# First norm's operands at the head of the weight queue, one branch around the overflow passes, and a two-pass last norm, in a four-layer fp32 network on one core

## The reference, cut to what matters

```python
# block 1, layer 0 begins with
h = x * rsqrt(mean(x * x) + 1e-6) * pre_mix_norm[0]     # first norm, 256 x 1024
proj = h @ w_in[0]                                       # 2464 columns
...
# block 2, layer 1 ends with (ALPHA = 4 ** 0.25)
top_val, top_idx = top_k(h @ router, 2)                  # 8 experts, 2 per token
gate = one_hot(top_idx) weighted by softmax(top_val)
y = 0
for e in range(8):
    y += gate[:, e] * ((silu(h @ w_gate[e]) * (h @ w_up[e])) @ w_down[e])   # 1024 -> 3584 -> 1024
z = ALPHA * h + y
out = (z - mean(z)) * rsqrt(var(z) + 1e-5) * ln_g + ln_b
```

## Time and profile before

| | |
|---|---|
| three executions, median | 2643.1 us (2642.37, 2643.1, 2655.18) |
| profiled execution | 2652.31 us, its span 2650.5 us |
| mean granted TensorE clock | 0.958 |
| PE, PEld, DVE, ACT, POOL busy | 93%, 51%, 18%, 15%, 4% |
| moved by DMA | 568 MB, mean 214 GB/s |
| the expert layer in the span | 1640 to 2618 us |

### The profile page before, as it was taken

The page is one execution under the profiler, slowest core; times in us unless marked ns, Lnnn a source line. Parts: engine busy times, 40 slices in busy tenths (PEclk is TensorE's granted clock), DMA queues, the critical chain, the costliest instruction groups (busy, mean ns, idle before and its releaser), DMA issues. The chain is left out here.

```text
span 2650.5 us, 34369 instructions
## 1 busy us (share of the span) xinstructions
PE 2475.4 (93%) x14986; PEld 1340.9 (51%) x14987; DVE 488.7 (18%) x1219; ACT 398.8 (15%) x967; POOL 110.3 (4%) x189
## 2 busy tenths in 40 slices
PE   6899999999999599999977997999999999999994
PEld 3577774678774264867546744333333333333331
DVE  2340004240001441200102513111111110101112
ACT  0420001330000142100011521111111111011110
POOL 3110000000000020000000100000000000000000
PEclk9999999799999789999975998999999999999997
DMA  8558543433343244243433233999999999999991
GB/s 268 196 65 213 199 143 118 178 105 137 133 145 113 68 136 174 104 161 109 130 103 123 70 136 130 357 384 355 350 354 391 334 358 367 359 368 357 367 361 54
DMA packets 247242, 568.11 MB, mean 214 GB/s; under 512 B 10224, under 2 KB 25776, under 8 KB 247088
## 3 DMA queue, kind: packets, MB, share of 16 engines
q1 hardware_dynamic: 234992, 531.71, 55.0%
q0 software_dynamic: 12096, 34.12, 5.8%
HBM read 556.62 MB, written 9.18 MB: 213 GB/s over the span
## 5 line engine op out<-in xcount | busy, mean ns | idle before, releaser
L1241 PE MATMUL ps_d<-slots,hT 128*32 128x512 f32 x3584 | 391.8, 593 | 0.1
L867 PE MATMUL ps_a<-slots,hT 128*128 128x512 f32 (+4 forms) x672 | 276.4, 569 | 17.6 <-ACT hT L1477 9.9
L1241 PEld LDWEIGHTS ps_d<-slots,hT 128*32 128x32 f32 x3584 | 112.7, 110 | 257.5 <-issue 257.1
L1268 PE MATMUL ps_x<-slots,PT 128*32 128x512 f32 x1792 | 213.0, 593 | 0.8 <-ACT PT L1633 0.8
L867 PEld LDWEIGHTS ps_a<-slots,hT 128*128 128x128 f32 x672 | 127.1, 196 | 160.1 <-issue 145.0
L1241 PE MATMUL ps_s<-slots,hT 128*32 128x512 f32 x1792 | 197.4, 592 | 0.0
L1054 PE MATMUL ps_a<-hT,slots 128*128 128x256 f32 x864 | 191.0, 379 | 1.9 <-issue 1.9
L1054 PE MATMUL ps_d<-hT,slots 128*128 128x256 f32 x864 | 190.9, 379 | 0.0
L1054 PEld LDWEIGHTS ps_a<-hT,slots 128*128 128x128 f32 x864 | 163.8, 190 | 29.5 <-issue 8.0
L1054 PEld LDWEIGHTS ps_d<-hT,slots 128*128 128x128 f32 x864 | 164.2, 190 | 22.3
L2278 DVE TENSOR_TENSOR proj<-proj,ps_d 128x512 f32<-128x512 f32 x33 | 22.7, 687 | 595.4 <-PE ps_d L1054 521.4
(11 more groups left out here) (350 smaller groups left out, 2263.8 us busy)
## 6 DMA issues: line engine op xcount, KB each, us to landing
slots<-in_moe_w_gate SPq DMA_DIRECT2D x56, 2048.0 KB, 9.6
slots<-in_moe_w_up SPq DMA_DIRECT2D x56, 2048.0 KB, 10.6
slots<-in_moe_w_down SPq DMA_DIRECT2D x56, 2048.0 KB, 11.2
slots<-in_ffn_w_gate_up SPq DMA_DIRECT2D x20, 2048.0 KB, 9.7
slots<-in_ffn_w_down SPq DMA_DIRECT2D x10, 2048.0 KB, 8.4
slots<-in_w_in SPq DMA_DIRECT2D x8, 2048.0 KB, 9.7
slots<-in_ff_w_gate SPq DMA_DIRECT2D x5, 2048.0 KB, 7.9
slots<-in_ff_w_up SPq DMA_DIRECT2D x5, 2048.0 KB, 7.8
```

Source lines behind the costliest of these rows:

```text
L867: last = pe.matmul(b[:, 0:c], lhs[:, k, t * P:(t + 1) * P], v[:, k, :], start=(k == 0), stop=(k == s["k"] - 1))
L1241: last = pe.matmul(b[TILE * j:TILE * j + TILE, :], x_of[i][:, k, TILE * c:TILE * c + TILE], views[w][:, k, :], start=(k == 0), stop=(k == ...
L1268: last = pe.matmul(b0[TILE * j:TILE * j + TILE, :], mine(f + o, c), v[:, f + o, 512 * half:512 * half + 512], start=(first and o == 0), st ...
```

## The change

Four edits. (1) SP issues the first norm's gain between the two tiles of x, with a semaphore of its own; GpSimd keeps only the identity ahead of a wait for weight block 0, and issues all its tables behind that wait. (2) BODY becomes 1; the count read is the maximum over the eight experts, and one branch stands around a loop of eight turns, so that either all experts run both overflow passes or none does. (3) O begins as ALPHA X instead of zero; this is written behind the counts instead of ahead of them. (4) `last_norm` takes its statistics straight from O, of both tiles before the first normalising pass, and does the rest in two passes of 512-column halves, (O - mean) * gain and then * inverse root + shift; SP stores each half when it is done.

```diff
-BODY = 2
+BODY = 1
...
+        most = loads[0:1, EXPERTS:EXPERTS + 1]          # loads is one column wider
...
             for t in range(T):                            # SP
                 sp.dma_start(X[:, t, :], a["x"][0, t * P:(t + 1) * P, :])...
+                if t == 0:
+                    sp.dma_start(vec[:, 0, :], vectors[0].unsqueeze(0).broadcast_to([P, D])).then_inc(
+                        *lane.tick(first_vec_landed, ("vec", 0), by=16))
...
-                with lane.loop(sp, 2) as turn:
-                    for u in range(BODY):
-                        ...
-                        n = sp.value_load(loads[0:1, bass.ds(e, 1)], min_val=0, max_val=S)
-                        with sp.If(n > FIRST):
-                            for groups in passes:
-                                expert(e, groups)
-                        with sp.Else():
-                            ...
+                start = dict(lane.count)
+                n = sp.value_load(most, min_val=0, max_val=S)
+                with sp.If(n > FIRST):
+                    with lane.loop(sp, 2) as e:
+                        for groups in s["groups"]:
+                            expert(e, groups)
+                with sp.Else():
+                    added = {sem.name: count for sem, count in lane.since(start)}
+                    for n in range(s["first"] - SLOTS, s["first"]):
+                        landed = slot_landed[n % SLOTS]
+                        sp.wait_ge(*lane.of(("weights", n)))
+                        sp.sem_inc(landed, added[landed.name])
             for t in range(T):
-                sp.wait_ge(*lane.of(("last", t)))
-                sp.dma_start(out[0, t * P:(t + 1) * P, :], X[:, t, :])...
+                for c in (0, 512):
+                    sp.wait_ge(*lane.of(("last", t, c)))
+                    sp.dma_start(out[0, t * P:(t + 1) * P, c:c + 512], X[:, t, c:c + 512])...
...
                 pool.dma_start(ident[:, :], a["c_ident"])...
-                pool.dma_start(vec[:, 0, :], vectors[0].unsqueeze(0).broadcast_to([P, D]))...
+                pool.wait_ge(*lane.of(("weights", 0)))
                 for dst, src in ((onehot, a["c_bucket"]), ...
...
             def last_norm(s):
-                g, b = use_vec(s["gain"]), use_vec(s["shift"])
+                g, shift = use_vec(s["gain"]), use_vec(s["shift"])
                 dve.wait_ge(*lane.own())
-                for t in range(T):
-                    do(dve.scalar_tensor_tensor(X[:, t, :], X[:, t, :], ALPHA, O[:, t, :], ALU.mult, ALU.add))
+
+                def moments(t):
                     for c in range(2):
-                        do(dve.bn_stats(stat[:, 36 + 6 * c:42 + 6 * c], X[:, t, 512 * c:512 * c + 512]))
+                        do(dve.bn_stats(stat[:, 36 + 6 * c:42 + 6 * c], O[:, t, 512 * c:512 * c + 512]))
                     do(dve.bn_aggr(stat[:, 32 + 2 * t:34 + 2 * t], stat[:, 36:48]))
-                    inv_root(1, stat[:, 33 + 2 * t:34 + 2 * t], 1.0, LN_EPS)
-                    do(dve.tensor_scalar(X[:, t, :], X[:, t, :], stat[:, 32 + 2 * t:33 + 2 * t], stat[:, 0:1],
-                                         ALU.subtract, ALU.mult))
-                    do(dve.tensor_tensor(X[:, t, :], X[:, t, :], g, ALU.mult), ("vec_used", s["gain"]))
-                    do(dve.tensor_tensor(X[:, t, :], X[:, t, :], b, ALU.add), ("vec_used", s["shift"]), ("last", t))
+
+                moments(0)
+                r = start_root(1, stat[:, 33:34], 1.0, LN_EPS)
+                moments(1)
+                for t in range(T):
+                    for c in (0, 512):
+                        o, x = O[:, t, c:c + 512], X[:, t, c:c + 512]
+                        post(dve.scalar_tensor_tensor(x, o, stat[:, 32 + 2 * t:33 + 2 * t], g[:, c:c + 512],
+                                                      ALU.subtract, ALU.mult), ("vec_used", s["gain"]))
+                    end_root(1, r)
+                    for c in (0, 512):
+                        x = X[:, t, c:c + 512]
+                        post(dve.scalar_tensor_tensor(x, x, stat[:, 0:1], shift[:, c:c + 512], ALU.mult, ALU.add),
+                             ("vec_used", s["shift"]), ("last", t, c))
+                    if t == 0:
+                        dve.wait_ge(*lane.own())
+                        r = start_root(1, stat[:, 35:36], 1.0, LN_EPS)
...
-                do(dve.memset(O[:, :, :], 0.0))
                 b, n = bank(lane, "d")                     # route_tokens
                 dve.wait_ge(*lane.of(("full", "d", n)))
...
-                do(dve.tensor_copy(loads[:, :], b[:, 16:24]), ("free", "d", n), ("loads", 0), sem=d_free)
+                do(dve.tensor_copy(loads[:, 0:EXPERTS], b[:, 16:24]))
+                do(dve.tensor_reduce(loads[:, EXPERTS:EXPERTS + 1], b[:, 16:24], AX, ALU.max), ("free", "d", n),
+                   ("loads", 0), sem=d_free)
+                for t in range(T):
+                    post(dve.tensor_scalar(O[:, t, :], X[:, t, :], ALPHA, None, ALU.mult))
...
                 elif kind == "experts":                    # VectorE; TensorE and ScalarE likewise
-                    with lane.loop(dve, 2) as turn:
-                        for u in range(BODY):
-                            start, before = dict(lane.count), lane.own()
-                            tokens = dve.value_load(loads[0:1, bass.ds(turn * BODY + u, 1)], min_val=0, max_val=S)
-                            with dve.If(tokens > FIRST):
-                                for first, groups in zip(s["starts"], s["groups"][2 * u:2 * u + 2]):
-                                    expert(groups, first, turn * BODY + u)
-                            with dve.Else():
-                                dve.wait_ge(*before)
-                                for sem, count in lane.since(start):
-                                    dve.sem_inc(sem, count)
+                    start, before = dict(lane.count), lane.own()
+                    tokens = dve.value_load(most, min_val=0, max_val=S)
+                    with dve.If(tokens > FIRST):
+                        with lane.loop(dve, 2) as e:
+                            for first, groups in zip(s["starts"], s["groups"]):
+                                expert(groups, first, e)
+                    with dve.Else():
+                        dve.wait_ge(*before)
+                        for sem, count in lane.since(start):
+                            dve.sem_inc(sem, count)
```

More of the change, by code:

```diff
@@ L1429, in _ @@
                 elif kind == "experts":
-                    with lane.loop(pe, 2) as turn:
-                        for u in range(BODY):
-                            start, before = dict(lane.count), lane.own()
[L1433 to L1438, removed]
-                                for sem, count in lane.since(start):
-                                    pe.sem_inc(sem, count)
+                    start, before = dict(lane.count), lane.own()
+                    tokens = pe.value_load(most, min_val=0, max_val=S)
+                    with pe.If(tokens > FIRST):
+                        with lane.loop(pe, 2) as e:
+                            for groups in s["groups"]:
+                                expert(groups)
+                    with pe.Else():
+                        pe.wait_ge(*before)
+                        for sem, count in lane.since(start):
+                            pe.sem_inc(sem, count)
                 elif kind == "route":
@@ L1739, in _ @@
                 elif kind == "experts":
-                    with lane.loop(act, 2) as turn:
-                        for u in range(BODY):
-                            start, before = dict(lane.count), lane.own()
-                            tokens = act.value_load(loads[0:1, bass.ds(turn * BODY + u, 1)], min_val=0, max_val=S)
-                            with act.If(tokens > FIRST):
-                                for groups in s["groups"][2 * u:2 * u + 2]:
-                                    expert(groups)
-                            with act.Else():
-                                act.wait_ge(*before)
-                                for sem, count in lane.since(start):
-                                    act.sem_inc(sem, count)
+                    start, before = dict(lane.count), lane.own()
+                    tokens = act.value_load(most, min_val=0, max_val=S)
+                    with act.If(tokens > FIRST):
+                        with lane.loop(act, 2) as e:
+                            for groups in s["groups"]:
+                                expert(groups)
+                    with act.Else():
+                        act.wait_ge(*before)
+                        for sem, count in lane.since(start):
+                            act.sem_inc(sem, count)
                 leave(lane, n)
```

26 lines of the change are left out of this document (7 added, 19 removed).

## The result

The changed kernel takes **2630.8 us** in the median of 13 executions (2618.2 to 2645.2), the kernel before 2643.1 in 13 (2640.8 to 2660.3). The measured ratio is 0.9924 with a 95% interval of 0.9904 to 0.9944, so it is faster, by 0.76% in this measure. This ratio, like those of the experiments, is not the quotient of the two medians, which is 0.9953 here. The forecast was 2619.7, with a range of 2612 to 2632. The profiled execution takes 2631.24, its span is 2629.4; before they were 2652.31 and 2650.5. Span against span that is -21.1 us, median against median -12.3. The difference between these two is the main thing to explain.

The account below looks back on a forecast made before the run. TensorE was taken to bound the expert layer, so only start, routing and end could change: -8.0 + 1.8 - 12.0 - 4.6 - 0.6 = -23.4 us off the median of 2643.1, giving 2619.7 us, range 2612 to 2632.

Parts of the forecast that it names:

- Rival (b): Whole kernel: the changed median falls with the highest executions, 2631.8 us, not told from no change; chance 0.10.
- Start: Kernel start: with the tables behind weight block 0, that block lands at 13.0 us and TensorE starts earlier, -8.0 us.
- The cover for GpSimd: After the start: GpSimd's tables and biases shift by 10.5 us, and a further delay below 14 us costs nothing.
- rival (d): Start: the tables slow weight block 1, TensorE stands again after the first product, 4 us, 2623.7 us; chance 0.05.
- Routing: Ahead of the experts' gather: a reduction and two scalings added behind the counts, +1.8 us.
- 1 more: Routing: 1 us more if half of TensorE's longer standing cost again as slow matmuls.
- rival (c): Routing into expert layer: TensorE's clock stays low longer, for 60 us giving 2649.7 us, so slower; chance 0.03.
- Branches: End, VectorE's loop of empty experts: one turn left instead of eight, the norm starts earlier, -12.0 us.
- norm: Last norm: statistics of both tiles, then eight passes over 512 columns, 9.4 us instead of 14.01, -4.6 us.
- tail: After the last norm, final store: the last piece is 256 KB instead of 512 KB, -0.6 us.
- What is late ahead of it moves its end one to one: Ahead of the expert layer: time gained or lost there moves that layer's end by the same amount.
- anywhere that it did not: Whole kernel: a new wait of TensorE for weights would show the prediction wrong; no size given.

Follow-up runs that it names:

- E1: The kernel before, unchanged, run again for the scatter of its executions: 2648.5 us, ratio 0.9989.
- E9: The changed kernel, nothing edited, in its third set of executions: 2619.2 us, ratio 0.9875 against the kernel before.
- E5: The changed kernel, nothing edited, run again beside the kernel before: 2637.8 us, ratio 0.9949.
- E3: The changed kernel with ALPHA X written ahead of the wait for the counts: 2629.5 us, ratio 0.9923 against the kernel before.
- E4: The changed kernel with the 6 MB line store cut into eight pieces spread over the first ffn: 2639.0 us, ratio 0.9917 against the kernel before.
- E7: The changed kernel without GpSimd's wait for weight block 0, the gain still on SP: 2640.4 us, ratio 0.9949 against the kernel before.

## Why the prediction was right, and where not

**Direction and mechanism.** Five terms made -23.4; the traces give -22.6 for the same five. The pair most alike is E1 and E9, which show no fall of the clock in either attention and the same mean clock:

```profile
core 0: 2641.4 us, clock 0.962
```

```profile
core 0: 2616.9 us, clock 0.962
```

They are 24.5 us apart. Not all of that is the change's, as the first ffn shows, E1 first, then E9:

```profile
260.98 8.83 PE L1054 MATMUL ps_a<-hT,slots 128*128 128x256 f32 x32 [2.69 <-issue]
```

```profile
249.38 7.14 PE L1056 MATMUL ps_a<-hT,slots 128*128 128x256 f32 x32 [1.23 <-issue]
```

There E1 loses 3.2 us more, to a longer wait and a half clock that either kernel can have or not. Without them the pair is 21.3 apart, like the -21.1 of the two first profiles.

**The base was the step that failed.** The prediction took the terms off the median of three, on the ground that "the terms do not depend on which execution it is". That is true of the terms and not of the base. The executions don't scatter about one value. E1 has a clock of 1.00 from 490 to 540 us, the profile of before 0.73 in the same stretch with the same code, and its span is 9.1 longer. Such a fall occurs or not in the second attention and in the first (100 to 140 us); what decides it is not shown. Of the three times of before, 2642.4, 2643.1 and 2655.2, two lie where E1's profile without a fall lies; over 106 executions the median is 2653.6, and the terms taken off it give 2630.2, where 2630.8 was measured. The -12.3 between the medians is small for the same reason: of the 13 executions of before, seven lie within 5 us of the shortest, of all 106 only 35, and of the changed kernel's first 13 only three. The profiled execution was the better base: 2652.3 - 23.4 = 2628.9 stood in the prediction, 1.9 from the median measured. Rival (b), the median falling high at 2631.8, came out in its number, though not in its verdict of no change: the interval excludes 1. So the direction and the sizes of the terms came out as they were worked out. That the median fell inside 2612 to 2632 owes something to luck: it is 11.1 above the forecast, in the part of the range that was added to take in the rivals.

**Start.** Forecast -8.0, measured -7.5, with block 0 landed at 13.6 instead of 13.0: from 3 to 7 us only 308 GB/s moved, where I took 393. The cover for GpSimd held: the last neighbourhood bias is there at 80.8, and nobody waits for it. Block 1 did not stop TensorE, so rival (d) falls. The 1 us lost again before the stage "lines" is the first product, whose 32 matmuls take 15.69 us instead of 14.68; in E5 the same code takes 14.13, so it is not the change's.

**Routing.** The fills cost 1.2 instead of 1.6, the slow matmuls 1.2, which the prediction named as a possible "1 more" and left out of its sum. E3 and the traces with it show that the wait comes from where the fill stands. The matmuls are slower in all seven traces with the late fill than in the three with the memset (5.79 to 5.98), but an early fill did not reliably give that back. The clock is at 1.00 from 1635 on, so rival (c) did not occur.

**Branches, norm, tail.** -12.8: the one jump that is left takes 0.56, like the 0.52 of the earlier trace rows, and I had added 0.6 for a dearer jump and the way to the norm. The prediction had combined the rule of the Trainium skill, page "Runtime: NRT & Kernel Launch", section "Instruction fetch mechanics", with the longer jump of the earlier trace rows and so had 1.16 as a second value for it. The jump took 0.56, and E5 and E9 have 2.14 us from the last add to the norm too, so that size is not borne out; whether the 0.56 is such a fetch no run shows. The prediction's 3.4 us for a turn of ScalarE was a misreading, without consequence. ScalarE's increments behind each empty expert, before and after:

```profile
L1750 ACTq EVENT_SEMAPHORE  x8: 17/17/17, 2620.7 to 2628.4; - x8
```

```profile
L1750 ACTq EVENT_SEMAPHORE  x1: 17/17/17, 2617.1 to 2617.1; - x1
```

The eight turns are 1.1 us apart; most of the 27.55 us was one wait for VectorE's last add (`L1672`, 18.88 us from 2600.4 on). So ScalarE is through at 2617.1 and not near 2606, just ahead of VectorE's norm at 2617.28. The norm is 0.3 short because a half pass is 0.71. The tail is exact.

**Ahead one to one?** "What is late ahead of it moves its end one to one" holds for the expert layer: the changed kernel is 3.4 us ahead at its start and 3.4 at its end. Ahead of it the lead is not carried whole, from 8.1 us at 120 to 5.5 at 265. The prediction named a wait of TensorE for weights as what would prove it wrong "anywhere that it did not". In the first ffn it had waited already, in rows that I had not read: 1.9 and 2.69 us in two traces of before, 2.90, 2.66 and 1.23 in three of the changed kernel. These overlap, and one trace of each kernel has the half clock behind the wait, so neither can be laid to the change; E4 shows what both come from. How often the clock falls in the attentions with one start or the other stays open.

## What to carry to other kernels

Before adding terms to a median of few executions, read whether executions differ by stretches of low clock, and compare traces that agree in them; else 10 us of such stretches stand for or against a change of 20. Span times granted clock told the start's gain from zero where the times could not. Keep narrow table loads behind the first weight block: what costs is their running beside it, not their bytes; no run issued them from another queue. Work placed where TensorE waits for it is paid as the wait, and the matmuls behind it can run at the low clock besides.

## What the runs showed of the hardware

- The same program has the granted clock at 1.00 all through an attention or in part at 0.50, from execution to execution: 2641.4 against 2650.5 us for the kernel before, 2616.9 against 2637.0 for the changed one. The Trainium skill, page "TensorE: Matmul & The Clock Gate", section "What's actually happening", says that the chip's measuring of TensorE's activity runs freely and does not start anew with the kernel. That fits; no run here shows that it is the cause.
- 14 small loads of 0.70 MB, and four of 0.8 KB behind them, took the DMA engines from 395 GB/s (changed kernel, 7 to 13.6 us) to 232 (E7, 7 to 17 us), both at a busy share of over 1.0. They cost 7.4 us, where their bytes would be 1.8.
- Two stores of together 6 MB, read from 16 and 8 partitions and issued one behind the other, had landed after 88 us (46.1 and 87.0 each); from 150 to 200 us the DMA engines were busy 0.95 at 122 GB/s.
- Two posted scalings of 1024 columns and the start of what follows take 1.21 us, 0.6 each, where the nearest single instruction, with two operations instead of one, takes 0.81.
- A pass over 512 columns takes 0.71 us where one over 1024 takes 1.22 to 1.28, so halving a pass does not halve its time.
